# Sums of squares over heads in retention and local attention: one fp32 product each, or two single-pass products of a high part and a remainder

## What is computed

```python
h = rms(x) ; z = h @ w_in                       # split among the mixers and four gates
merged = sum_i sigmoid(gate_i) * (mixer_i(z) @ P_i)     # stick-breaking, retention, RWKV-7, local attention
x += merged @ w_o
x += relu(rms(x) @ w_up)**2 @ w_down

def _rms(x, g=None, eps=EPS):
    y = x * rsqrt(mean(x * x, axis=-1) + eps)
    return y if g is None else y * g
```

## Time and profile before

| | us |
|---|---|
| median of 3 runs | 1216.63 (1214.82 to 1216.95) |
| the profiled execution, as timed | 1213.98 |
| its span, first to last instruction | 1212.2 |
| TensorE busy | 1180.3 (97%) |
| DVE, ACT, POOL busy | 504.2 (42%), 489.4 (40%), 468.8 (39%) |

### The profile page before, as it was taken

The page is one execution under the profiler, slowest core; times in us unless marked ns, Lnnn a source line. Parts: engine busy times, 40 slices in busy tenths (PEclk is TensorE's granted clock), DMA queues, the critical chain, the costliest instruction groups (busy, mean ns, idle before and its releaser), DMA issues.

```text
span 1212.2 us, 21083 instructions
## 1 busy us (share of the span) xinstructions
PE 1180.3 (97%) x8974; PEld 973.9 (80%) x8974; DVE 504.2 (42%) x1001; ACT 489.4 (40%) x808; POOL 468.8 (39%) x288
## 2 busy tenths in 40 slices
PE   8999999999999899999999999999899999999998
PEld 7998877887788588667777777789888888888886
DVE  4799435455554544443453676361522000222000
ACT  6455323232223444775726534423543312344220
POOL 3443435325442234323323622433344544344541
PEclk9999999999999999999999999999999999999999
DMA  6222323222221142212522312323122323232330
GB/s 248 88 73 84 115 80 111 69 70 93 98 78 54 35 147 81 64 35 68 193 74 77 104 41 70 138 89 105 53 95 97 122 93 98 71 103 97 112 122 35
DMA packets 35855, 111.49 MB, mean 92 GB/s; under 512 B 4257, under 2 KB 8865, under 8 KB 35250
## 3 DMA queue, kind: packets, MB, share of 16 engines
q1 hardware_dynamic: 30144, 98.59, 24.6%
q10 hardware_dynamic: 5106, 11.43, 2.6%
q0 software_dynamic: 512, 0.13, 0.1%
HBM read 99.43 MB, written 9.04 MB: 89 GB/s over the span
## 4 chain that ended last, share of the span: by engine, by line
PE 81%; DVE 10%; ACT 5%; POOL 2%; issue 2%; DMA 0%; DVEq 0%; ACTq 0%
PE pst L1803 18%; PE pst L1805 17%; PE pst L1804 17%; PE pst L1992 5%; PE pst L1993 5%; PE pst L1994 5%; POOL w_lo L799 1%; PE pst L2314 1%; ACT w_hi L917 1%; PE pst L2306 1%; DVE x_lo L1663 1%; PE pst L2092 1%; PE pst L2039 1%; PE pst L2276 1%; PE pst L2291 1%
## 5 line engine op out<-in xcount | busy, mean ns | idle before, releaser
L799 POOL TENSOR_TENSOR w_lo<-raw,w_hi 128x1024 fp32r<-128x1024 f32 x164 | 402.6, 2461 | 642.4 <-ACT w_hi L917 630.7
L1803 PE MATMUL pst<-h_hi,w_hi 128*128 128x512 f32 (+1 forms) x704 | 255.9, 363 | 1.3 <-DVE h_lo L1369 0.7
L1805 PE MATMUL pst<-h_hi,w_lo 128*128 128x512 f32 (+1 forms) x704 | 243.2, 345 | 0.0
L1804 PE MATMUL pst<-h_lo,w_hi 128*128 128x512 f32 (+1 forms) x704 | 242.9, 345 | 0.0
L917 ACT ACTIVATE w_hi<-raw 128x1024 fp32r<-128x1024 f32 x164 | 171.3, 1051 | 147.7 <-PE pst L1994 114.2
L1803 PEld LDWEIGHTS pst<-h_hi,w_hi 128*128 128x128 f32 x704 | 133.4, 189 | 25.3 <-issue 4.7
L1805 PEld LDWEIGHTS pst<-h_hi,w_lo 128*128 128x128 f32 x704 | 133.3, 189 | 15.9
L1804 PEld LDWEIGHTS pst<-h_lo,w_hi 128*128 128x128 f32 x704 | 133.6, 190 | 15.1 <-issue 2.2
L1803 PE MATMUL pst<-x_hi,w_hi 128*128 128x512 f32 (+1 forms) x272 | 102.7, 377 | 3.8 <-POOL w_lo L799 2.0
L1805 PE MATMUL pst<-x_hi,w_lo 128*128 128x512 f32 (+1 forms) x272 | 102.4, 377 | 0.0
L1804 PE MATMUL pst<-x_lo,w_hi 128*128 128x512 f32 (+1 forms) x272 | 102.4, 376 | 0.0
(11 more groups left out here) (338 smaller groups left out, 2062.9 us busy)
## 6 DMA issues: line engine op xcount, KB each, us to landing
raw<-in_weights SPq DMA_DIRECT2D x164, 512.0 KB, 3.4
xt<-in_x SPq DMA_DIRECT2D x4, 512.0 KB, 5.4
wait_gate<-stage ACTq DMA_DIRECT2D x8, 256.0 KB, 2.7
gate_t<-wait_gate ACTq DMA_DIRECT2D x1, 2048.0 KB, 9.0
x<-in_x ACTq DMA_DIRECT2D x1, 2048.0 KB, 7.8
out<-x SPq DMA_DIRECT2D x8, 256.0 KB, 3.1
cst<-in_consts SPq DMA_DIRECT2D x1, 1524.0 KB, 11.1
wait_ret_g<-stage ACTq DMA_DIRECT2D x4, 256.0 KB, 3.0
```

Of the source, the lines that this page charges most:

```text
L799: nc.gpsimd.tensor_tensor(w_lo[:, u % W_SLOTS, :], raw[:, u % RAW_SLOTS, :], w_hi[:, u % W_SLOTS, :].bitcast(F32), ALU.subtract).then_inc( ...
L1803: M(out, lh, rh, start=(first and i == 0), stop=False)
L1804: M(out, lh, rl, start=False, stop=False)
L1805: last = M(out, ll, rh, start=False, stop=(final and i == len(terms) - 1))
```

## The change

The products of squares are made from two fp32r operands, as in the dense products. ACT squares a tile and then copies the square to fp32r, DVE subtracts the copy from the square to get the remainder (a new step, `sw_square` and `ret_square` in DVE's program), and TensorE multiplies the matrix with the high part and with the remainder into the same bank. `headsum` in fp32r is a new copy made by ACT at the start of retention, in a place where a mask of stick-breaking attention stood; `neg_ones` in fp32r existed. The local squares have one buffer for the squares and one for their high parts instead of two for squares, so ACT's square of tile i waits for the multiplication of tile i - 1 instead of i - 2. The place of the local square in the order moves behind one of the two pieces for b = 1 to 4.

```diff
@@ placements
+        rsq_hi = place("ret_sq_hi", [P, 2, T], F32R, at=[at[0]])
...
+        rsq_lo = place("ret_sq_lo", [P, 2, T], F32R, at=[at[0]])
         rsq = place("ret_sq", [P, 2, T], at=at)
...
-        dsq = place("sw_sq", [P, 2, L], at=[table_at])
+        dsq_lo = place("sw_sq_lo", [P, L], F32R, at=[table_at])
+        dsq = place("sw_sq", [P, L], at=[table_at])
+        dsq_hi = place("sw_sq_hi", [P, L], F32R, at=[table_at + 4 * L])
@@ run_after_rw
             for b in range(NB + 1):
                 g("ret_scores", b)
+                if b:
+                    pieces(1)
                 g("sw_square", b)
-                pieces(RET_FILL[b][0])
+                pieces(RET_FILL[b][0] - (1 if b else 0))
                 g("ret_out", b)
@@ ACT
             def ret_gate():
+                act.wait_ge(o_done, 4)
+                A(sb_mask_r[:, 0:P], headsum, ACT.Copy)
                 use_tables("exp_and_others")
...
-                A(rsq[:, h % 2, :], ro[:, h, :], ACT.Square).then_inc(rsq_ready, 1)
+                link(A(rsq[:, h % 2, :], ro[:, h, :], ACT.Square))
+                A(rsq_hi[:, h % 2, :], rsq[:, h % 2, :], ACT.Copy).then_inc(sq_ready, 1)
...
-                if i >= 2:
-                    act.wait_ge(dn_ready, i - 1)
-                A(dsq[:, i % 2, 0:n], src, ACT.Square).then_inc(dsq_ready, 1)
+                if i:
+                    act.wait_ge(dn_ready, i)
+                link(A(dsq[:, 0:n], src, ACT.Square))
+                A(dsq_hi[:, 0:n], dsq[:, 0:n], ACT.Copy).then_inc(sq_ready, 1)
@@ DVE
+            def sw_square(i):
+                n = T if i else L
+                dve.wait_ge(sq_ready, i + 1)
+                V.tensor_tensor(dsq_lo[:, 0:n], dsq[:, 0:n], dsq_hi[:, 0:n].bitcast(F32), ALU.subtract)\
+                    .then_inc(sq_split, 1)
+
+            def ret_square(h):
+                dve.wait_ge(sq_ready, NB + 1 + h + 1)
+                V.tensor_tensor(rsq_lo[:, h % 2, :], rsq[:, h % 2, :], rsq_hi[:, h % 2, :].bitcast(F32), ALU.subtract)\
+                    .then_inc(sq_split, 1)
@@ TensorE
             def ret_sum(h):
-                pe.wait_ge(rsq_ready, h + 1)
-                M(pst[:, 4 + h % 2, :], C("neg_ones"), rsq[:, h % 2, :], start=True, stop=True).then_inc(rss_done, 1)
+                pe.wait_ge(sq_split, NB + 1 + h + 1)
+                M(pst[:, 4 + h % 2, :], sb_mask_r[:, P:2 * P], rsq_hi[:, h % 2, :], start=True, stop=False)
+                M(pst[:, 4 + h % 2, :], sb_mask_r[:, P:2 * P], rsq_lo[:, h % 2, :], start=False, stop=True)\
+                    .then_inc(rss_done, 1)
...
             def sw_sum(i):
-                pe.wait_ge(dsq_ready, i + 1)
+                pe.wait_ge(sq_split, i + 1)
                 if i:
                     pe.wait_ge(drs_ready, i)
-                    last = M(pst[:, 3, :], headsum, dsq[:, i % 2, 0:T], start=True, stop=True)
+                    M(pst[:, 3, :], sb_mask_r[:, 0:P], dsq_hi[:, 0:T], start=True, stop=False)
+                    last = M(pst[:, 3, :], sb_mask_r[:, 0:P], dsq_lo[:, 0:T], start=False, stop=True)
                 else:
                     for hf in range(2):
-                        last = M(pst[:, 1 + 2 * hf, 0:HL], headsum, dsq[:, 0, HL * hf:HL * hf + HL],
-                                 start=True, stop=True)
+                        cols = slice(HL * hf, HL * hf + HL)
+                        M(pst[:, 1 + 2 * hf, 0:HL], sb_mask_r[:, 0:P], dsq_hi[:, cols], start=True, stop=False)
+                        last = M(pst[:, 1 + 2 * hf, 0:HL], sb_mask_r[:, 0:P], dsq_lo[:, cols], start=False, stop=True)
```

More of the change, by code:

```diff
@@ L476, in build @@
             sem("ro_done"), sem("ro_ready"))
-        rsq_ready, rss_done, rrs_ready, ry_ready = sem("rsq_ready"), sem("rss_done"), sem("rrs_ready"), sem("ry_ready")
-        dsq_ready, dss_done, drs_ready, dn_ready, dk2_in = (
-            sem("dsq_ready"), sem("dss_done"), sem("drs_ready"), sem("dn_ready"), sem("dk2_in"))
+        sq_ready, sq_split = sem("sq_ready"), sem("sq_split")
+        rss_done, rrs_ready, ry_ready = sem("rss_done"), sem("rrs_ready"), sem("ry_ready")
+        dss_done, drs_ready, dn_ready, dk2_in = (
+            sem("dss_done"), sem("drs_ready"), sem("dn_ready"), sem("dk2_in"))
         ds_done, ds_read, dmx_ready, dexp_ready, dp_ready, dpt_done, dpt_act, dpt_dve, do_done = (
@@ L1185, in sw_square @@
                     act.wait_ge(sw_in, 32)
-                if i >= 2:
-                    act.wait_ge(dn_ready, i - 1)
-                A(dsq[:, i % 2, 0:n], src, ACT.Square).then_inc(dsq_ready, 1)
+                if i:
+                    act.wait_ge(dn_ready, i)
+                link(A(dsq[:, 0:n], src, ACT.Square))
+                A(dsq_hi[:, 0:n], dsq[:, 0:n], ACT.Copy).then_inc(sq_ready, 1)
             def sw_norm(i):
-                sq = dsq[:, i % 2, 0:T if i else L]
+                sq = dsq[:, 0:T if i else L]
                 act.wait_ge(dss_done, i + 1)
@@ L1596, in sw_norm @@
                 V.scalar_tensor_tensor(out=y, in0=y, scalar=gain_q[:] if i else PAR("kn", 0),
-                                       in1=dsq[:, i % 2, 0:T if i else L], op0=ALU.mult, op1=ALU.mult)\
+                                       in1=dsq[:, 0:T if i else L], op0=ALU.mult, op1=ALU.mult)\
                     .then_inc(dn_ready, 1)
+            def sw_square(i):
[7 more added lines that the diff above has]
+                    .then_inc(sq_split, 1)
             def sw_keys():
@@ L1788, in _ @@
                 ret_scores=ret_scores, ret_out=ret_out, ret_norm=ret_norm, sw_norm=sw_norm, sw_keys=sw_keys,
+                sw_square=sw_square, ret_square=ret_square,
                 sw_scores=sw_scores, sw_probs=sw_probs, sw_turn=sw_turn, sw_out=sw_out,
```

## The result

| | before | after |
|---|---|---|
| median of 5 runs, us | 1216.63 (1214.32 to 1217.14) | 1221.08 (1219.95 to 1221.89) |
| profiled execution as timed, us | 1213.98 | 1219.95 |
| its span, us | 1212.2 | 1218.2 |

The ratio is 1.0042 with a 95% interval of 1.0028 to 1.0057: 5.1 us (3.4 to 6.9). The forecast was +2.8 us, 1219.4. The direction is right and 1221.1 lies in the range, but the loss is about 2 us larger than forecast.

The account below looks back on a forecast made before the run. TensorE, busy for 97% of the span, was taken to bound the kernel. Delay at block 2's transposes less later savings, +4.8 - 2.0 = +2.8 us, on the median 1216.63 gave 1219.4 us; range 1216.5 to 1222.8 us.

Parts of the forecast that it names:

- The place: ACT's square of b = 1 falls behind the last stick-breaking gate's tables and tanh, at 601.0 instead of 590.72.
- DVE held by POOL: DVE's subtraction for b = 1, asked at 602.35, is held by a POOL operation and ends at 604.05.
- Rival 2: POOL does not hold DVE's subtraction, which takes 0.69 us: +1.8 us, 1218.4 us; chance 0.12.
- The two waits: TensorE waits 3.15 us at the sum of b = 1, then 2.2 us for state updates before block 2's transposes.
- The keys' sum: Sum of the keys' squares (b = 0): four single-pass products save 0.41 us, of which about 0.2 to 0.3 counts.
- The five savings behind it: Sums of local tiles 2, 3, 4 and retention heads 0 and 1 on TensorE's path: 5 x 0.40 = 2.0 us saved.
- Heads 2 and 3: Their retention sums stand beside an ACT and DVE chain: no gain, the local scores wait grows 0.8 us.
- Rivals 3 and 4: 3: ACT's square of b = 1 in time, -2.7 us, chance 0.12; 4: more subtraction waits, +4.9 us, chance 0.12.
- rival 3: ACT's square of b = 1 is in time, so the first sum does not wait: -2.7 us, 1213.9 us; chance 0.12.
- the clock: TensorE's clock behind the two new waits: sum assumed no fall; a fall to 1.2 GHz would lose 2.8 us.
- rival 1: TensorE's clock falls in the new wait at b = 1: +2.8 + 2.8 = +5.6 us, 1222.2 us; chance 0.16.
- the forecast case: Late square of b = 1 and its waits, less later savings, at full clock: within 0.7 us of +2.8; chance 0.48.

Follow-up runs that it names:

- the square in PSUM: Changed kernel with ACT writing the square of b = 1 to a free PSUM bank for DVE's subtraction: 1219.39 us beside 1216.23, ratio 1.0025.
- the first experiment: Changed kernel with only the square of b = 1 back ahead of the piece: 1213.46 us beside 1216.23 for the kernel before, ratio 0.9985.
- the control: The changed kernel timed once more, nothing altered, against the kernel before: 1220.45 us beside 1216.31, ratio 1.0042.
- all squares ahead: Changed kernel with all five local squares in their old place ahead of both pieces: 1214.43 us beside 1216.03 for the kernel before, ratio 0.9992.
- the order only: Kernel before with only the local squares' order changed, sums in fp32, no copy or subtraction: 1216.40 us beside 1216.23, ratio 1.0001.

## Why the prediction was right in direction and short in size

- **The place.** Right. The count of pieces put the square of b = 1 behind the last stick-breaking gate, and it stands there (600.41; 601.0 was forecast). Putting it back ahead of the piece, or ahead of the tables, turns the loss into a gain.
- **DVE held by POOL.** Right: asked at 601.71 and done at 603.48, for 602.35 and 604.05 forecast. Rival 2 falls, and the square in PSUM shows what it would have given: 1.1 us on this wait (2.98 to 1.85), for 1.0 forecast, and 2.1 us by the ratios, as less is lost to the clock too.
- **The two waits.** Right, 3.0 and 1.7 us for 3.15 and 2.2. The transposes of block 2 come at +4.0, or +4.4 against a trace that was 0.4 us early from the start, for +4.8 forecast.
- **The keys' sum.** Better than I took it: the saving is the whole 0.4 us (next instruction at 588.46 for 589.24, of which 0.4 belongs to the early start), not 0.2 to 0.3. DVE's subtraction ended at 586.95 and its updates at 588.1, 0.8 us ahead of my working, of which 0.4 is again the early start.
- **The five savings behind it.** Right: from +6.5 behind block 2's outputs to +4.5 at the gate is 2.0 us.
- **Heads 2 and 3.** Right: +4.48 at the gate on ACT and +4.49 at the chain's return. The scores wait grew to the 2.1 us forecast, and taking these two changes back costs nothing. That the longer wait could itself bring the clock down was not thought of.
- **Rivals 3 and 4.** No other sum waits, and this order is not faster; rival 3's mechanism is what the first experiment runs: 1.8 us faster, for 2.7 forecast, with 0.5 us lost to the new wait for `ret_kd`. Its trace also has the fall of the clock behind the scores wait.
- **The step that failed: the clock.** The sum took TensorE at the full clock behind the waits, "by the rows alone, which show no fall behind the 1.3 us wait ... it stays +2.8", and gave the fall a chance of 0.16. It was wrong to let a wait of 1.3 us speak for two of 3.15 and 2.2 us: the only rows that showed TensorE after a longer idle time, those at the start of the span, were at half rate. The trace of before has waits of 1.80 and 1.96 us near 855 and 869 with no fall behind them, and other traces have falls behind these very waits, so one trace could not have ruled the fall out. The term belonged in the sum with its own price: forecast in the rival as 2.8 us, measured 2.5 us in the trace, 3.2 us by the filled waits. So the measured loss is that of rival 1 (chance 0.16) on waits a little shorter than forecast, and not the forecast case, which ended at +3.5; it lies in the range because the range took in that rival.

With the terms as measured, the trace gives +4.0 + 2.5 - 2.0 = +4.5 us by the chain's return. The medians differ by 4.45 us, the ratio says 5.1 (3.4 to 6.9), the control's medians 4.1. The traced execution's further 1.5 us are the fall of the clock near 859; the traced execution of before had no fall between 100 and 1200 us.

## What to carry to other kernels

Before an instruction is moved behind "one piece of work", list what each engine does in that piece at that very place: three of the four moves here made no wait, and the fourth put the square behind 6.3 us of tables and tanh. A consumer on a second in-order engine doubles such a mistake, since what is queued behind the waiting instruction becomes late in its turn. On TensorE a wait of some 3 us should be priced as the wait plus a stretch at half rate, unless a row of the same kernel shows the full clock behind a wait of that length: in all three traces with the 3.0 us wait the clock fell in it or behind it. And the same change, with one square put in time, is a small gain (ratios of 0.9980 to 0.9985), so it pays to ask which part of a losing change loses.

## What the runs showed of the hardware

- Needless matmuls in a wait made the kernel faster: 20 products of 480 columns in the two waits, 3.2 us less by the ratios, granted clock 1.00 from 606 to 612 where it had been 0.50 from 606 to 610. The mean granted clock was recorded for every execution, traced or not, and it agrees: on average 0.9972 for the kernel before (77 executions beside the experiments), 0.9943 for the changed one (11), 0.9972 with the waits filled (11). The difference of 0.0029 is 3.5 us of the span, at most, since time at half rate in which TensorE waits costs nothing.
- The fall of the clock is not the same in every execution. With the same waits it came at 602 to 604 in one trace of the changed kernel and after 604 in the other. Behind the unchanged wait of 1.80 us near 859 it came in the traces of four kernels (the changed one, all squares ahead, the square in PSUM, the square ahead of the tables) and was absent in the others, among them the second trace of the changed kernel. Two of the others (the order only, heads 2 and 3 in fp32) have a fall behind the next wait, 1.96 us for a weight near 869, which all kernels have too; three have one behind the 2.1 us wait at the scores. The traces of before, of the filled waits and of the subtraction behind the state updates have no fall at these three places. Here are the windows of the stretch near 859 in the changed kernel's first trace:

```profile
860.00:862.00 2.00, 2.00 (x13) 2.00 (x12) 2.00 (x8) 0.86 (x4) 0.00 (x0) 0.61 0.03 8
862.00:864.00 2.00, 2.00 (x11) 2.00 (x11) 0.02 (x1) 0.00 (x0) 0.00 (x0) 0.53 0.00 0
```

  It cost 1.5 us there (+4.5 before it, +6.0 behind). Runs of one kernel differ by 2 to 4 us, and the clock goes with most of that. Of the 77 executions of the kernel before, the 11 with a mean granted clock of 0.999 have a median of 1213.9 us, the 29 with 0.996 one of 1217.1 us. These are 3.2 us apart, where 0.003 of the span is 3.6 us. The traced execution of before, 2.65 us under its median, had 0.999.
- A DVE operation with two SBUF inputs can be stretched a long way by POOL: 1.77 and 2.77 us instead of 0.69 and 0.75. With one operand in PSUM it kept its 0.69 us beside the same POOL work.
